# Loading, first norm and first projection of a two-layer block in one block of instructions

## The reference

```
h = x * rsqrt(mean(x*x, over features) + 1e-6) * ln1_w
p = h @ w_in                       # 1024 -> 3488 columns
p[:, :1920] -> RWKV mixer          # p + mu * (0.5*(prev + next) - p) first
p[:, 1920:] -> gated linear attention (q, k, v, two gates of 16 columns, output gate)
x = x + mix @ w_out
```

## Time and profile before

| | us |
|---|---|
| three runs, median | 2873.42 |
| lowest, highest | 2868.87, 2874.36 |
| the profiled execution, its own time | 2873.28 |
| its span | 2871.3 |
| TensorE busy | 2468.6 (86% of the span) |
| VectorE busy | 1274.8 (44%) |
| ScalarE busy | 584.9 (20%) |
| GpSimd busy | 205.8 (7%) |

### The profile page before, as it was taken

How to read it: one execution, slowest core, us unless ns; L and a number is a source line. 1 busy time by engine, 2 the same in 40 slices (tenths; PEclk the granted TensorE clock), 3 DMA queues, 4 the chain that set the end, 5 groups by cost and what they waited for, 6 DMA issues and landing times. The chain is left out here.

```text
span 2871.3 us, 42464 instructions
## 1 busy us (share of the span) xinstructions
PE 2468.6 (86%) x18496; PEld 1514.9 (53%) x18496; DVE 1274.8 (44%) x2101; ACT 584.9 (20%) x850; POOL 205.8 (7%) x142
## 2 busy tenths in 40 slices
PE   4996399978999999899765978898989788989897
PEld 2785299957545455378223844343436474434343
DVE  4777756654323233288666331112127742112112
ACT  3333501113111111153501221000012340101001
POOL 2000000113000000020143110000000030000000
PEclk7998589988999999999877989999999898999999
DMA  4581122324799999635110459999973056999996
GB/s 152 164 284 63 37 84 84 92 73 165 333 406 417 417 416 417 264 132 167 38 44 1 185 229 426 428 428 428 427 313 91 30 207 274 427 428 428 428 427 257
DMA packets 121289, 725.85 MB, mean 253 GB/s; under 512 B 11958, under 2 KB 65462, under 8 KB 84087
## 3 DMA queue, kind: packets, MB, share of 16 engines
q1 hardware_dynamic: 92920, 695.79, 60.1%
q10 hardware_dynamic: 28224, 27.92, 2.9%
HBM read 721.58 MB, written 2.10 MB: 252 GB/s over the span
## 5 line engine op out<-in xcount | busy, mean ns | idle before, releaser
L2048 PE MATMUL ps<-s_ring,s_c_XG 128*64 128x512 f32 x2048 | 473.7, 619 | 83.5 <-DMA s_ring<-in_exp_w 65.6
L2048 PEld LDWEIGHTS ps<-s_ring,s_c_XG 128*64 128x64 f32 x2048 | 164.3, 142 | 387.0 <-issue 385.9
L2160 DVE TENSOR_TENSOR s_c_hid<-ps,s_c_sil 128x512 f32<-128x512 f32 x32 | 34.3, 1072 | 517.7 <-PE ps L2048 517.7
L2089 PE MATMUL ps<-s_ring,s_c_hidT 128*64 128x512 f32 x1024 | 223.5, 594 | 0.0
L2048 PE MATMUL ps<-s_ring,s_m_XG 128*64 128x512 f32 x1024 | 222.9, 593 | 0.0
L2048 PEld LDWEIGHTS ps<-s_ring,s_m_XG 128*64 128x64 f32 x1024 | 72.9, 137 | 142.6 <-issue 141.5
L2089 PEld LDWEIGHTS ps<-s_ring,s_c_hidT 128*64 128x64 f32 x1024 | 72.2, 137 | 137.5 <-issue 136.5
L358 PE MATMUL ps<-s_h_part,s_w_hi 128*128 128x512 f32 x368 | 117.8, 402 | 24.8 <-PEq L479 20.4
L358 PE MATMUL ps<-s_src_part,s_w_hi_at 128*128 128x512 f32 x384 | 126.4, 412 | 0.6 <-DVE s_src_part L1598 0.6
L2172 DVE SCALAR_TENSOR_TENSOR s_c_Y_lo<-ps,s_c_w_slot,s_c_Y_hi 128x512 fp32r<-128x512 f32 x32 | 22.6, 746 | 211.8 <-ACT s_c_Y_hi L2129 211.8
L2089 PE MATMUL ps<-s_ring,s_m_hidT 128*64 128x512 f32 x512 | 113.4, 596 | 0.0
(11 more groups left out here) (629 smaller groups left out, 4427.2 us busy)
## 6 DMA issues: line engine op xcount, KB each, us to landing
s_ring<-in_exp_w SPq DMA_DIRECT2D x192, 2048.0 KB, 17.3
s_ring<-in_moe_w_gate SPq DMA_DIRECT2D x32, 2048.0 KB, 12.2
s_ring<-in_moe_w_up SPq DMA_DIRECT2D x32, 2048.0 KB, 15.1
s_ring<-in_moe_w_down SPq DMA_DIRECT2D x32, 2048.0 KB, 12.3
s_mod_w_at<-in_vectors SPq DMA_DIRECT2D x58, 512.0 KB, 4.2
s_mod_w<-in_vectors SPq DMA_DIRECT2D x54, 512.0 KB, 4.6
s_w_raw<-in_w_in ACTq DMA_DIRECT2D x11, 1024.0 KB, 7.6
s_w_raw_at<-in_w_in ACTq DMA_DIRECT2D x8, 1024.0 KB, 5.9
```

The lines of the kernel that those rows point to most:

```text
L2048: last = nc.tensor.matmul(ps[x * SLOTS:(x + 1) * SLOTS, bank + fh, :], XG[:, k, c0:c0 + SLOTS], w[x][:, at:at + 512], start=(k == 0), stop ...
L2089: last = nc.tensor.matmul(ps[rows, DOWN + half, :], hidT[:, f, rows], w[x][:, at:at + 512], start=(f == 0), stop=(f == nj - 1))
L2160: nc.vector.tensor_tensor(hid_out[:, fh * per:(fh + 1) * per, :], ps[:, UP + fh, :].rearrange("s (p j) -> s p j", j=nj), sil[:, fh * 512:( ...
```

## The change

The three blocks ahead of the projection go, and their work moves into the projection's block. `rows` now lies in `mix`. SP loads the first half of the rows, `base`, `vec`, the small gate weights, one modulation job with its c row, the masks, then the other modulation rows; ACT loads the second half of the rows, weight units 0 and 1 and `w_gl`. The squares are summed token-major (two quarters on VectorE, two on ACT, with an accumulator), so mean, root and reciprocal have 4 columns. The reciprocal goes into four diagonal matrices, and the product of the rows with these turns and scales them at once. ACT takes the high parts straight from PSUM with the weight `ln1_w` as scale, VectorE the low parts. The first two tiles are made together, slice by slice, as the parts arrive. "gl" is made from split parts in three passes. `xT` is filled by plain transposes of the rows in eight new tiles of kind "x", in pairs after t2, t3, t4 and t5; the four z tiles come behind them, before t6.

```diff
-        def load_and_transpose(dram, dst, n_tok, first):
...
-        def rms_norm(src, dst, n_tok, weight, shift=None, sq=None, parts=None, ahead=None):
...
+            turns = [(None, 0, "x", c) for c in range(KD)]
             tiles[2:2] = [(None, 0, "gl", 0)]
-            tiles[5:5] = [(None, d, "z", c) for d in range(2) for c in range(2)]
-            gl_at, z_end = 2, 8
+            for n in range(KD // 2):
+                tiles[4 + 3 * n:4 + 3 * n] = turns[2 * n:2 * n + 2]
+            tiles[15:15] = [(None, d, "z", c) for d in range(2) for c in range(2)]
+            gl_at, z_end = 2, 18
...
-                room = [{"rwkv": 3, "qk": 6, "v": 3, "og": 6, "gl": 0, "z": 0}[kind] for _, _, kind, _ in tiles]
+                room = [{"rwkv": 3, "qk": 6, "v": 3, "og": 6, "gl": 0, "z": 0, "x": 0}[kind] for _, _, kind, _ in tiles]
...
                     @block.sync
                     def _(sp):
-                        sp.dma_start(gw2[:], A["gla_gw2"]).then_inc(gw_here.sem, 16)
-                        M.load(sp)
+                        sp.dma_start(rows[:, 0:2, :], x_rows[:, 0:2, :]).then_inc(rows_here[0].sem, 16)
+                        sp.dma_start(base[:], A["consts"][:, 0:const_at["base_end"]]).then_inc(*inputs_in.up(16))
+                        sp.dma_start(vec[:], A["vectors"][:, 0:n_vec]).then_inc(*inputs_in.up(16))
+                        sp.dma_start(gw2[:], A["gla_gw2"]).then_inc(small_here.sem, 16)
+                        M.load(sp, 0, 1)
+                        sp.dma_start(masks[:], masks_in).then_inc(small_here.sem, 16)
+                        M.load(sp, 1)
...
                     @block.tensor
                     def _(pe):
+                        for j in range(2):
+                            pe.wait_ge(rows_here[j].sem, 16)
+                        pe.wait_ge(*diag_done.at(1))
+                        for d in range(KD):
+                            for t in range(KT):
+                                last = nc.tensor.matmul(ps[:, d, t * P:(t + 1) * P], rows[:, t, d * P:(d + 1) * P], diag[:, t, :], start=True, stop=True)
+                            last.then_inc(*turned.up())
+                        W.ready(pe, 0)
+                        for last in W.product_pair([ps[:, 0, :], ps[:, 1, :]], 0, parts, slice(0, T), lambda k: pe.wait_ge(*x_lo.at(max(k + 1, 2)))):
+                            last.then_inc(*mm_done.up())
                         for i, (u, j, kind, idx) in enumerate(tiles):
+                            if i < 2:
+                                continue
...
                             if kind == "gl":
-                                pe.wait_ge(inputs_in.sem, l0 + 16)
-                                for k in range(KD):
-                                    last = nc.tensor.matmul(ps[0:32, i % 8, :], w_gl[:, k, :], hT[:, k, :], start=(k == 0), stop=(k == KD - 1))
+                                pe.wait_ge(*gl_split.at(2))
+                                passes = [(k, a, b) for k in range(KD) for a, b in ((0, 0), (0, 1), (1, 0))]
+                                for n, (k, a, b) in enumerate(passes):
+                                    last = nc.tensor.matmul(ps[0:32, i % 8, :], gl_parts[a][:, k, :], parts[b][:, k, :], start=(n == 0), stop=(n == len(passes) - 1))
+                            elif kind == "x":
+                                for t in range(KT):
+                                    last = nc.tensor.transpose(ps[:, i % 8, t * P:(t + 1) * P], rows[:, t, idx * P:(idx + 1) * P], ident)
...
                     @block.scalar
                     def _(act):
+                        act.dma_start(rows[:, 2:4, :], x_rows[:, 2:4, :]).then_inc(rows_here[1].sem, 16)
+                        W.load(act, 0, 2)
+                        act.dma_start(w_gl[:], w[:, :, gl0:gl0 + 32]).then_inc(small_here.sem, 16)
+                        act.wait_ge(*warmed.at(1))
+                        nc.scalar.activation(warm[:], warm[:], ACT.Sqrt)
+                        act.wait_ge(rows_here[1].sem, 16)
+                        for t in range(2, KT):
+                            nc.scalar.activation(spare[t], rows[:, t, :], ACT.Square, accum_out=total[:, t:t + 1]).then_inc(*squared.up())
+                        act.wait_ge(*ms_done.at(1))
+                        nc.scalar.activation(root[:], ms[:], ACT.Sqrt).then_inc(*root_done.up())
+                        W.split_hi(act, 0)
+                        act.wait_ge(inputs_in.sem, 32)
+                        for k in range(KD):
+                            act.wait_ge(*turned.at(k + 1))
+                            nc.scalar.activation(parts[0][:, k, :], ps[:, k, :], ACT.Copy, scale=vcol("ln1_w", k)).then_inc(*x_hi.up())
+                        W.split_hi(act, 1)
+                        act.wait_ge(small_here.sem, 48)
+                        nc.scalar.activation(gl_parts[0][:], w_gl[:], ACT.Copy).then_inc(*gl_split.up())
...
-                        W.load(act, W.next_unit(), 2)
-                        act.dma_start(w_gl[:], w[:, :, gl0:gl0 + 32]).then_inc(*inputs_in.up(16))
                         M.silu_of_c(act)
-                        for u in range(W.next_unit(), 2):
-                            W.split_hi(act, u)
                         W.load_unit(act, 2)
...
+                            elif kind == "x":
+                                ins = nc.scalar.activation(xT[:, idx, :], src, ACT.Copy)
...
                     @block.vector
                     def _(dve):
-                        for u in range(W.next_unit(), 2):
-                            W.split_lo_unit(dve, u)
+                        V = nc.vector
+                        V.memset(warm[:], 1.0).then_inc(*warmed.up())
+                        dve.wait_ge(rows_here[0].sem, 16)
+                        for t in range(2):
+                            ins = V.tensor_tensor_reduce(spare[t], rows[:, t, :], rows[:, t, :], 1.0, 0.0, ALU.mult, ALU.add, total[:, t:t + 1])
+                        vlink(ins)
+                        dve.wait_ge(*squared.at(2))
+                        V.tensor_scalar(ms[:], total[:], 1.0 / D, RMS_EPS, ALU.mult, ALU.add).then_inc(*ms_done.up())
+                        dve.wait_ge(*root_done.at(1))
+                        vlink(V.reciprocal(rstd[:], root[:]))
+                        dve.wait_ge(inputs_in.sem, 32)
+                        V.tensor_tensor(diag[:], bcast(ident, KT), rstd[:].unsqueeze(2).to_broadcast([P, KT, P]), ALU.mult).then_inc(*diag_done.up())
+                        W.split_lo_unit(dve, 0)
+                        for k in range(KD):
+                            dve.wait_ge(*x_hi.at(k + 1))
+                            V.scalar_tensor_tensor(parts[1][:, k, :], ps[:, k, :], vcol("ln1_w", k), parts[0][:, k, :].bitcast(F32), ALU.mult, ALU.subtract).then_inc(*x_lo.up())
+                        W.split_lo_unit(dve, 1)
+                        dve.wait_ge(small_here.sem, 48)
+                        dve.wait_ge(*gl_split.at(1))
+                        V.tensor_tensor(gl_parts[1][:], w_gl[:], gl_parts[0][:].bitcast(F32), ALU.subtract).then_inc(*gl_split.up())
...
-        load_and_transpose(A["x"], xT, T, True)
...
-                with nc.Block() as block:
-                    @block.sync
-                    def _(sp):
-                        sp.dma_start(mk[:], A["consts"][:, const_at["base_end"] + 1:]).then_inc(*inputs_in.up(16))
-                        sp.wait_ge(inputs_in.sem, l0 + 16)
...
-                        hT = mix
+                        rows = mix[:].rearrange("p (t h) n -> p t (h n)", h=2)
...
-                        rms_norm(xT, hT, T, lambda k: vcol("ln1_w", k), parts=parts, ahead=W)
```

More of the change, by code:

```diff
@@ L254, in build @@
         stored = signal("stored")
+        norm_squared = signal("norm_squared")
+        norm_summed = signal("norm_summed")
+        norm_sums_here = signal("norm_sums_here")
+        norm_ms = signal("norm_ms")
+        norm_root = signal("norm_root")
+        norm_diag = signal("norm_diag")
+        norm_spread = signal("norm_spread")
+        norm_dst = signal("norm_dst")
+        norm_hi = signal("norm_hi")
+        norm_lo = signal("norm_lo")
         def vlink(ins):
@@ L558, in square_weights, with project_first @@
             return SplitWeights(None, [[(0, w[:, :, c:c + UNIT_COLS])] for c in range(0, D, UNIT_COLS)], at)
-        def project_first(W, hT, parts, proj, gla_q, gla_k, gla_v, gla_gl, gla_og, sums, back, reset, jobs):
+        def project_first(W, rows, masks, masks_in, parts, proj, gla_q, gla_k, gla_v, gla_gl, gla_og, sums, back, reset, jobs):
             w, spans = w_first, first_spans
@@ L2449, in _ @@
                             last.then_inc(ctx_turned.sem, 1)
-                        pe.wait_ge(sums_here.sem, 1)
+                        pe.wait_ge(*sums_here.at(1))
                         for t in range(KT):
@@ L3229, in build @@
                     with ExitStack() as first:
[L3230 removed]
```

(2 more changed lines are left out.)

126 lines of the change are left out of this document (26 added, 100 removed).

## The result

The kernel after took 2852.68 us (median of four runs, 2849.98 to 2858.68) against 2873.89 for the kernel before: a ratio of 0.9936, 95% interval 0.9919 to 0.9954. The medians differ by 21 us; the ratio stands for 18 (13 to 23). The forecast was 29 us, 2844.3, with 2837.0 to 2851.5 as its range. The sign and most of the mechanism were right; the time lies 1.2 us above the range, and the start of the product and the length of the tail were sized wrong.

What follows compares the result with a forecast made beforehand. TensorE paces the tile loop behind a serial head; VectorE's modulation rows end the stage. Start 27.8 + warm start 3.1 + gl 1.6 - x tiles 3.5 = 29.0 us off, giving 2844.3 us, range 2837.0 to 2851.5.

Steps and rivals of the forecast that it cites:

- "New waits" (6): Head and early loop: ACT waits for small loads before splitting w_gl; costed at nothing, with 10 us of cover.
- the start of 23.2: Head: the projection's first matmul starts at 23.2 instead of 51.0, 27.8 us earlier.
- Rival (a): Head: the weights land late, the product starts at 26.8 to 30, time 2847.9 to 2851.3; chance 0.18.
- signs of being wrong: ACT's first split after 18, small-load wait above 1 us, second low-half stall, low clock in loop, 34 modulations over 77 us.
- the share of the DMA engines: Head loads: weights get 40% of the bytes beside modulation rows; unit 0 lands at about 16.7, still covered by the turning.
- Turning: Head: 32 products with a diagonal, 64 instructions, the first at half pace, ending at 23.1; bounds 21 to 28.
- Warm start: First projection tile: TensorE comes from the turning without a pause, so 3.1 us go.
- gl: The "gl" tile in the loop: 24 fp32r matmuls take 5.44 instead of 7.05 us, 1.6 gained.
- x tiles: Tile loop: x is turned among the tiles by 32 transposes, 0.44 us a tile, 3.5 lost.
- The stall in the loop: TensorE's wait for VectorE's low half: 4.6 us again, two tiles later, costed at nothing; bounds 6.3 gained, 3 lost.
- The tail: End of the stage: 74 us follow VectorE's start of t14 in either kernel, with 34 modulation jobs behind it.
- rival (c): Behind t14: the tail stretches, half of the 29 us comes back as longer DMA waits, 2858.8; chance 0.06.

Runs made afterwards that it cites:

- e1: Kernel after, with the load of w_gl moved from ACT's queue to SP's, behind the masks: 2841.67 us, ratio 0.9908.
- e3: Kernel after, with weight units 0 and 1 loaded on SP behind vec and w_gl left on ACT: 2840.85 us, ratio 0.9901.
- e2: Kernel after, with w_gl issued on ACT in front of weight units 0 and 1: 2848.97 us, ratio 0.9927.
- e7: As e1, but SP issues gw2, the modulation rows, masks and w_gl only once weight unit 0 has landed: 2838.66 us, ratio 0.9904.
- e9: Kernel after, with only weight unit 1 moved to SP behind vec; unit 0 and w_gl stay on ACT: 2841.96 us, ratio 0.9901.
- e4: As e1, with four buffers instead of three for modulation rows; diag, w_gl, gw2 laid into still empty tiles: 2834.9 us, ratio 0.9890.
- e6: Kernel after, with weight units 0 and 1 on SP, four modulation buffers, room 3 for x tiles, z work at t14: 2823.56 us, ratio 0.9850.
- e10: As e6, but with VectorE's work on the z tiles back at t7: 2827.56 us, ratio 0.9851.

## Why the prediction was right, and where it was wrong

**The bound and the mechanism: right.** The head was serial, the tile loop is paced by TensorE, and the stage ends with VectorE's rows behind t14. The earlier start went through the loop: the product moved by 19.6 us, t14 by 20.3 and the end of the stage by 17.7.

**Step that failed first: "New waits" (6), and the start of 23.2 with it.** "Everything is issued at once" put the issues at nothing, without a reason. I counted every wait on a semaphore on ACT and none for ACT's own issues, although four transfers, 3328 pieces, stood on its list in front of the first operation. The prediction said that ACT's sums run from 9.5 to 12.0; they ran from 18.0 to 20.2. e1 gives the size: the product starts at 23.69 instead of 31.44, 7.75 us, and the time is 8 us less. None of my rivals named this wait. Rival (a) looked at the landing of the same transfers and not at their issue; that its upper price, 2851.3, comes near the measured time is chance, since in the kernel after nothing waited for unit 0 to land. Two of the signs of being wrong did come up: ACT's first split of a weight unit was at 20.6, and there was a second stall on a low half.

That e1 starts the product at 23.69, close to the forecast 23.2, is partly luck too. Its diagonals were begun at 11.7 and the turning ended at 21.5, where the forecast had 13.0 and 23.1, so base and vec had landed earlier than I took; the pause of 2.24 for unit 0 filled the difference. With neither the stand nor the pause (e3) the product starts at 20.91.

**Step that failed second: the share of the DMA engines.** From the earlier trace rows I took 40% of the bytes for 1 KB pieces beside 4 KB ones. That window has 1217 packets on one queue and 437 on the other, and for some two of its ten us nothing moved at all: the queues were not both full in it, so it shows no share. Where both were full they moved piece for piece, 24% of the bytes in the kernel after, and in e1 unit 0 came at 18.0, past the 17.5 up to which the turning covers it. (Beside pieces of 4 KB, pieces of 1 KB get a fifth by count, not the quarter that the prediction worked with; SP's pieces averaged 3.2 KB, which makes it 24%.) The rule of the Trainium skill ("DMA: Bandwidth & Descriptors", "Queues, rings and completion order") that engines alternate by packets was the better guide; the trace agrees with an even count, 1280 and 1288. How many pieces an engine takes before it turns to the other queue, no run here shows. In the kernel after the small share was hidden behind ACT's late start; with that gone it costs 2.2 us.

**The other terms.** Turning: 64 instructions, as said, in 9.86 us (the forecast had 9.4). In the other ten kernels it took 8.7 to 10.2. Warm start: the first pair takes 11.0 us, from 31.44 to 42.44, without a slow stretch, as said. gl 5.55 for a forecast of 5.44. x tiles 0.90 a pair for 0.87. The stall in the loop 4.5 for 4.6, two tiles later than before; with the same loop it was 2.8 to 2.9 in e2, e3 and e7, so the match to 0.1 is luck. The forecast had t14 at 126.4 (155.43 - 29.0); from the true start of the product, 8.2 later, that is 134.7, and it was 135.09. So the sum behind the start was right within 0.4 us.

**The tail.** I took 74 us behind t14 as fixed; it was 76.7. That is rival (c) in small, 2.7 us. In the other kernels with three buffers and 34 rows (e1, e2, e3, e7, e9) it was 74.8, 75.1, 76.7, 75.6 and 77.6, so 74.0 of before lay at the low end, and I had read one execution as a constant. VectorE's waits for rows make up most of the difference, 20.5 us against 18.2. The e4 run shows what sets the length, the time from a freed buffer to a landed row; why that differs from kernel to kernel is not shown, and with one profile of each it cannot be told from the spread of executions.

**The sum, put right.** 29.0 - 8.2 (start) - 0.4 (between there and t14) - 2.7 (tail) = 17.7 at the end of the stage, as measured. The medians differ by 21.2; the 3.5 between lie outside this stage, in parts that were not changed, and the four runs of the kernel before alone span 6.3. Those 3.5 helped the forecast: the stage by itself would give 2855.6, 4 us above the range and not 1.2.

## What to carry to other kernels

Issuing is work of the engine that issues: add up the pieces of all transfers that stand in front of an engine's first operation, and give long lists of small pieces to an engine that has nothing else to do. When two queues are full at once, estimate shares by number of pieces, not by bytes, and read a share only from a window in which both are full. When a list of background jobs ends a stage, time it from several executions, and look first at how many transfers are in flight and at idle slots earlier in the list.

## What the runs showed of the hardware that I had not expected

A DMA issue can hold its engine for 11.36 us (w_gl in the kernel after), or two of them for 12.82 (the weight units in e2), where w_gl takes 0.44 to 0.50 with less in front of it (e1, e2, e3). What ended these stands can be counted. When the issue of w_gl ended at 16.6 in the kernel after, the transfers in front of it had 2304 pieces, of which 1046 had been moved: 1258 were left. In e2 at 14.6 it was 2304 - 1000 = 1304; for SP in e9 at 7.75, 1536 - 284 = 1252. That looks like room for some 1250 to 1300 pieces per queue in front of a new transfer. The other stands are not all so near. ACT's shorter one, at the transfer behind 1280 pieces, ended with 1154 to 1170 left (unit 1 in the kernel after and e1, w_gl in e9), and SP's at unit 1 in e3 with 1300. And in e3 SP's gw2 was through at 10.48 with 2560 - 778 = 1782 left, in e6 and e10 with 1770 and 1716, which does not fit at all; the cause was not settled. So what is shown is that an issue stands when well over a thousand pieces lie in front of it on its queue; a limit is not.

A product with a diagonal matrix in fp32 runs as two instructions per 128x128 piece at 0.115 us each at full clock, so turning and scaling together cost twice a plain transpose, and the whole vector work of the scaling is saved. The first tens of instructions ran at about half that pace here as well (64 in 9.86 us; ACT's first high parts come 1.64 us apart, the later ones 0.89), although the window from 21 to 31 lists a granted clock of 1.00.
